# Modulation chunks in pairs, and small transfers in five parts, inside the feed-forward stage of a hybrid diffusion trunk

## What is computed

```
for l in range(2):
    mod = silu(c) @ w_ada[l] + b_ada[l]          # 6 vectors of 2048: shift, scale, gate, twice
    h = rmsnorm(x, ng[0]) * (1 + sc_a) + sh_a
    o = concat(attention, conv, rwkv of h @ w_in[l]) @ w_out[l]
    x = x + g_a * rmsnorm(o, ng[1])
    h = rmsnorm(x, ng[2]) * (1 + sc_f) + sh_f
    ff = (silu(h @ w_gate[l]) * (h @ w_up[l])) @ w_down[l]     # 2048 -> 5632 -> 2048
    x = x + g_f * rmsnorm(ff, ng[3])
```

## Time and profile before

| what | value |
|---|---|
| median of 3 runs | 3166.36 us (3164.63 to 3168.65) |
| the profiled execution, device time | 3163.59 us |
| its span, first to last instruction | 3161.8 us |
| TensorE busy | 2880.3 us, 91% |
| VectorE, ScalarE busy | 1623.6 us (51%), 1113.9 us (35%) |
| DMA, mean over the span | 190 GB/s |
| feed-forward part of layer 0 | about 822 to 1640 us of the span |
| feed-forward part of layer 1 | about 2393 to 3090 us |

### The profile page before, as it was taken

One profiled execution on the slowest core, in us unless ns is written; L12 is line 12 of the kernel. 1 busy time (PEld: TensorE's weight loads), 2 busy tenths in 40 slices (PEclk: granted clock), 3 DMA queues, 4 the chain that ended last, 5 costly groups with the idle time before them and its releaser, 6 DMA issues. The chain is left out here.

```text
span 3161.8 us, 45973 instructions
## 1 busy us (share of the span) xinstructions
PE 2880.3 (91%) x17315; PEld 2168.0 (69%) x17315; DVE 1623.6 (51%) x2108; ACT 1113.9 (35%) x1441; POOL 165.6 (5%) x209
## 2 busy tenths in 40 slices
PE   6899788889699999999996998888898999999997
PEld 1578545568577777777875885555686888888885
DVE  0465544444545445444555655455445555555555
ACT  0344322224433333333434443222244444444442
POOL 1000111110000000000001001111100000000000
PEclk9999888889899999999997999888899999999998
DMA  9765556546366667666652656666454666666662
GB/s 365 244 179 160 190 202 214 194 156 193 103 218 215 219 215 221 217 218 216 188 165 78 183 154 201 206 219 211 158 173 129 191 186 187 190 187 189 188 187 93
DMA packets 317256, 600.86 MB, mean 190 GB/s; under 512 B 23184, under 2 KB 29288, under 8 KB 316584
## 3 DMA queue, kind: packets, MB, share of 16 engines
q1 hardware_dynamic: 309488, 592.90, 59.4%
q10 hardware_dynamic: 7608, 5.60, 0.6%
HBM read 595.28 MB, written 3.15 MB: 189 GB/s over the span
## 5 line engine op out<-in xcount | busy, mean ns | idle before, releaser
L826 PE MATMUL bank<-hiW,actH 128*128 128x512 f32 (+1 forms) x2304 | 906.3, 393 | 25.4 <-DVE loW L1331 23.2
L826 PE MATMUL bank<-hiW,actL 128*128 128x512 f32 (+1 forms) x2304 | 893.5, 388 | 0.0
L826 PE MATMUL bank<-loW,actH 128*128 128x512 f32 (+1 forms) x2304 | 893.5, 388 | 0.0
L1331 DVE TENSOR_TENSOR loW<-rawW,hiW 128x1024 fp32r<-128x1024 f32 x348 | 425.6, 1225 | 448.4 <-ACT hiW L408 448.2
L408 ACT ACTIVATE hiW<-rawW 128x1024 fp32r<-128x1024 f32 x348 | 368.0, 1060 | 570.1 <-PE bank L826 558.0
L826 PEld LDWEIGHTS bank<-hiW,actH 128*128 128x128 f32 x2304 | 435.7, 189 | 154.9 <-issue 63.2
L826 PEld LDWEIGHTS bank<-hiW,actL 128*128 128x128 f32 x2304 | 435.0, 189 | 89.8
L826 PEld LDWEIGHTS bank<-loW,actH 128*128 128x128 f32 x2304 | 435.6, 189 | 85.9 <-issue 1.0
L1726 DVE TENSOR_TENSOR loW<-rawW,hiW 128x1024 fp32r<-128x1024 f32 x244 | 298.9, 1225 | 376.1 <-ACT hiW L635 376.0
L635 ACT ACTIVATE hiW<-rawW 128x1024 fp32r<-128x1024 f32 x244 | 258.4, 1059 | 486.2 <-PE bank L826 486.2
L826 PE MATMUL bank<-rawW,csR 128*32 128x512 f32 x1536 | 327.8, 676 | 82.4 <-DMA rawW<-in_w_ada 35.0
(11 more groups left out here) (255 smaller groups left out, 2272.8 us busy)
## 6 DMA issues: line engine op xcount, KB each, us to landing
rawW<-in_w_ada SPq DMA_DIRECT2D x384, 512.0 KB, 5.8
rawW<-in_w_gate SPq DMA_DIRECT2D x176, 512.0 KB, 3.7
rawW<-in_w_up SPq DMA_DIRECT2D x176, 512.0 KB, 3.7
rawW<-in_w_down SPq DMA_DIRECT2D x176, 512.0 KB, 3.7
rawW<-in_w_in SPq DMA_DIRECT2D x144, 512.0 KB, 3.6
rawW<-in_w_out SPq DMA_DIRECT2D x64, 512.0 KB, 3.6
rawW<-in_w_in SPq DMA_DIRECT2D x16, 160.0 KB, 2.3
x<-in_x_prompt SPq DMA_DIRECT2D x1, 1024.0 KB, 6.9
```

The costliest lines, as they stand in the source:

```text
L826: return pe.matmul(out, a, b, start=start, stop=stop, skip_group_check=True)
L1331: TT(loW[:, slot, :, 0:width], rawW[:, slot, :, 0:width], hiW[:, c % LEAD, :, 0:width].bitcast(F32), ALU.subtract).then_inc(lo_ready, 1)
```

## The change

The modulation chunks of a block come in twos: a pair behind every sixth chunk, in place of one behind every third. A block has four pairs in place of eight single chunks; the products, their banks and their strips stay. `place`, the order of SyncE's loads, the order of TensorE's work and the count that VectorE waits for at the block's end follow. TensorE's wait for the row copied last (`rows_out`) moves from chunk 2 to chunk 5. Apart from that, `parameters` is cut into five parts, issued in blocks 2 to 6 between the conversions of chunks 15 and 16; at the start of layer 0 all five are issued one behind the other. The rule in `high` for the chunk four conversions back names the place in the block before, where j is over 1.

```
-            return ffn_base(l, j) * 4 + i + (i // 3 if ada_in(l, j) else 0)
+            return ffn_base(l, j) * 4 + i + (2 * (i // 6) if ada_in(l, j) else 0)
...
-                            if ada_in(l, j) and i % 3 == 2:
-                                a = i // 3
-                                load(0, place(l, j, i) + 1, wnext[:, 2 * a:2 * a + 2, (j - 1) * NW:j * NW])
+                            if ada_in(l, j) and i % 6 == 5:
+                                for a in range(2 * (i // 6), 2 * (i // 6) + 2):
+                                    load(0, place(l, j, i) + 1 + a % 2, wnext[:, 2 * a:2 * a + 2, (j - 1) * NW:j * NW])
...
-            def parameters(l):
-                act.wait_ge(prm_zero, l + 1)
+            def parameters(l, part):
...
+                if part == 0:
+                    act.wait_ge(prm_zero, l + 1)
...
-                        before = place(l, j, i - LEAD) if i >= LEAD else at - LEAD
+                        before = place(l, j, i - LEAD) if i >= LEAD else place(l, j - 1, i + FFN_CHUNKS - LEAD) if j > 1 else at - LEAD
...
-                        high(j, 12, 28)
+                        high(j, 12, 16)
+                        if 2 <= j < 7:
+                            parameters(l + 1, j - 2)
+                        high(j, 16, 28)
...
-                    parameters(l)
+                    for part in range(5):
+                        parameters(l, part)
...
-                if l + 1 < LAYERS:
-                    parameters(l + 1)
                 ffn(l)
...
-                    k = (2 * c if k0 is None else k0) + n
+                    k = 2 * c + n if k0 is None else k0 + 2 * (c - c0) + n
...
-                        if i % 3 == 2 and ada_in(l, j):
-                            if i == 2:
+                        if i % 6 == 5 and ada_in(l, j):
+                            if i == 5:
                                 pe.wait_ge(rows_out, 2 + 8 + (j - 1))
-                            ada_chunks(0, at + 1, at + 2, 6, 2 * (i // 3))
+                            ada_chunks(0, at + 1, at + 3, 6, 4 * (i // 6))
...
-                        dve.wait_ge(chunk_used, place(l, j, FFN_CHUNKS - 1) + 2 + SLOTS)
+                        dve.wait_ge(chunk_used, place(l, j, FFN_CHUNKS - 1) + 3 + SLOTS)
```

More of the change, by code:

```diff
@@ L441, in norm @@
                                    tf[:, b % 2].rearrange("p (k t) -> p k t", k=4), ACT.Copy).then_inc(nt_hi, 1)
-            def parameters(l):
-                act.wait_ge(prm_zero, l + 1)
+            def parameters(l, part):
+                row = lambda ap: ap.rearrange("(r c) -> r c", c=P)
                 put = lambda dst, src: act.dma_start(dst, src).then_inc(par_rows, 16)
-                row = lambda ap: ap.rearrange("(r c) -> r c", c=P)
+                tab = lambda dst, src: act.dma_start(dst, src).then_inc(par_tabs, 16)
@@ L447, in parameters @@
                 mu = A["rwkv_mu"][l]
[L448 to L468, removed]
+                if part == 0:
+                    act.wait_ge(prm_zero, l + 1)
+                    put(prm[0:12, 0, :], row(mu[0:12 * P]))
+                    put(prm[12:13, 0, 0:64], mu[12 * P:12 * P + 64].unsqueeze(0))
+                    put(prm[13:14, 0, 0:GATE_RANK], mu[12 * P + 64:D_RWIN].unsqueeze(0))
+                    for c, name in ((COL_W0, "rwkv_w0"), (COL_A0, "rwkv_a0")):
+                        put(prm[c:c + 8, 0, :], A[name][l].rearrange("d (r c) -> (d r) c", c=P))
@@ new lines, in parameters @@
+                if part == 1:
+                    for c, name in ((COL_KK, "rwkv_k_k"), (COL_KA, "rwkv_k_a"), (COL_LG, "rwkv_ln_g"), (COL_LB, "rwkv_ln_b")):
+                        put(prm[c:c + 4, 0, :], row(A[name][l]))
+                if part == 2:
+                    put(prm[COL_RK:COL_RK + 4, 0, :], A["rwkv_r_k"][l].rearrange("(r a) b -> r (a b)", a=2))
+                    put(prm[COL_CV:COL_CV + 12, 0, :], A["conv_w"][l].rearrange("w (r c) -> (w r) c", c=P))
+                    put(prm[0:64, 1, :], A["norm_g"][l].rearrange("n (r c) -> (n r) c", c=P))
+                    put(prm[0:96, 2, :], row(A["b_ada"][l]))
@@ new lines, in parameters @@
+                if part == 3:
+                    tab(wla[0:32], A["rwkv_w_up"][l].rearrange("d r n -> r d n"))
+                    tab(wla[32:64], A["rwkv_a_up"][l].rearrange("d r n -> r d n"))
+                    tab(wg[:], A["rwkv_g_up"][l])
+                    tab(ctxk[:], A["cache_k"][0][l])
+                    tab(ctxv[:], A["cache_v"][0][l])
+                if part == 4:
+                    tab(qkw[:, 0], A["q_norm"][l].partition_broadcast(P))
+                    tab(qkw[:, 1], A["k_norm"][l].partition_broadcast(P))
+                    for d in range(2):
+                        tab(s0all[:, d], A["state_rwkv"][0][l][d].rearrange("(f h) i j -> (h i) f j", h=2))
```

## The result

The changed kernel takes 3119.3 us (median of 4 runs, 3113.4 to 3121.7), the kernel before 3165.5 beside it; the ratio is 0.9851, with a 95% interval of 0.9834 to 0.9868, so 42 to 53 us less. The prediction was 3119.5 us in a range of 3112 to 3130.

The account below looks back on a forecast made before the run. The prediction took TensorE's own stream and its interruptions to bound layer 0's feed-forward part. Savings of 37.7 us (detours) and 9.2 us (transfers), 46.9 us, took 3166.4 us to 3119.5 us, range 3112 to 3130 us.

Parts of the forecast that it names:

- The bound: Layer 0's feed-forward part: TensorE's own stream and its interruptions, one 7.4 us wait and 64 detours, set the end.
- The detours: Layer 0's feed-forward blocks: 64 single-chunk detours of 1.197 us become 32 pairs of 1.217 us, saving 37.7 us.
- case of no overlap: Rival: a pair's second chunk runs wholly behind the first, 1.05 us more; 13.9 us saved, 3152.5 us; 3 in 100.
- rows of eight: Layer 0's earlier parts: two chunks together, eight records, span 1.06 and 1.07 us; the second costs 0.01 to 0.02 us.
- The partial overlap: Rival: in each pair the second chunk is held up 0.26 us; 8.4 us lost, 3127.9 us; 5 in 100.
- The transfers: Ahead of layer 0's feed-forward part: moving 22 small DMAs into blocks 2 to 6 removes a stall, 9.2 us saved.
- What else moves: Feed-forward part's load order, row copy, residues and earlier conversions: nothing gained or lost, 0 us.
- The slower rival: A pair's own weights land late and TensorE waits; at 20 us landing 96 us lost, 3215.5 us; 2 in 100.
- The sum: Whole kernel: 37.7 + 9.2 = 46.9 us saved from the median of 3166.4 us, giving 3119.5 us.

Follow-up runs that it names:

- e3_same_strips: Changed kernel, but pairs are chunks (0,2), (1,3), (4,6), (5,7), both writing the same two strips: 3146.2 us, ratio 0.9934 to the kernel before.
- the parts alone: Changed kernel with single modulation chunks again, transfers still in five parts: 3155.6 us, ratio 0.9965 to the kernel before.
- the pairs alone: Changed kernel with the 22 transfers again in one piece ahead of the feed-forward part: 3130.3 us, ratio 0.9885 to the kernel before.
- e6_narrow: Changed kernel with modulation products of 64 columns in place of 512 inside the feed-forward part: 3095.2 us, ratio 0.9766 to the kernel before.
- e5_one_place: Changed kernel with all 22 transfers issued in block 2, between conversions of chunks 15 and 16: 3118.4 us, ratio 0.9840 to the kernel before.
- e7_octets: Changed kernel with all eight modulation chunks of a block in one detour at its end: 3191.2 us, ratio 1.0075 to the kernel before.
- e4_quads: Changed kernel with four modulation chunks behind every twelve: 3113.4 us, ratio 0.9834 to the kernel before; run again, 3111.3 us.

## Why the prediction was right

**The bound.** TensorE's stream was taken as the only limit of the stage, and it is: in the changed kernel it is busy through every block at full granted clock, and it has no wait from 845 to 1560 us.

**The detours.** 1.197 us for a single chunk stood for 64 of them; a pair was put at 1.217 and takes 1.205. The gain, 32 x (2 x 1.197 - 1.205) = 38.0 us, was put at 37.7. What made it safe was that eight such records stood in the trace of before, in another stage. That the strips are the reason, and not only that detours are half as many, was an argument there; `e3_same_strips` shows it for 27.4 of the 38.0 us. The other 10.7 us, what half as many detours save as such, the prediction did not tell apart: its case of no overlap put a second chunk at a further 1.05 us (3152.5 us in all), where 0.86 and 3146.2 were measured. Its rows of eight held both gains, so the sum was right without it. The partial overlap, some 3127 us in the estimate from the Trainium skill's 2.38 for three column tiles, does not show: the four strips take 1.07 us together where two take 1.05. The span model of the same section (TensorE: Matmul & The Clock Gate, "Measured speedup vs the span model"), some 4 ns for a further tile, is close to these rows.

**The transfers.** 9.2 us were taken from the difference between the layers; the changed kernel's own is 34.38 - 25.04 = 9.3, and the parts alone gave 0.35% (0.23 to 0.47), 11 us with 7 to 15 in the interval. With the pairs alone the stall came out at 10.7 us, more than any estimate here, since the clock stayed low for longer behind it. That the issues cost nothing in their new place was argued from 2.88 us of idle time; it is shown, and with more room than was claimed: even 9.4 us of issues are hidden there.

**What else moves** was put at 0. That holds for the time. But one sentence of that step was incomplete: that a load starts as many chunks ahead as before. It does, and yet with pairs 14 conversions wait for their load, and modulation loads land after 5.8 us instead of 4.6. A likely reason is that two modulation loads start one right behind the other, and the weights behind them share the DMA engines with both; it is not shown apart, and the pace counts too: with pairs in the same order `e3_same_strips`, whose blocks are slower, has 3 such waits, `e6_narrow`, whose blocks are faster, 17. The slower rival was on the right track, weights that come late, with the wrong weights: it was priced by a pair's own, needed 17 us later, while what comes late first are feed-forward weights. With eight chunks in a detour late weights make the kernel slower than before.

**The sum** of 46.9 us stands against 46.2 in the stage and 46.2 between the medians (3165.5 - 3119.3). So close a match is partly luck. The two terms came out at 38.0 + 9.3 = 47.4 us, and the stage's moving end took 1.2 us back in the execution profiled, where the granted clock was low for longer behind a wait that both kernels have. Between the medians the interval is 42 to 53 us.

## What to carry to other kernels

Narrow products that leave strips of the array empty are cheapest where enough of them stand together to fill all strips: here a second chunk cost 0.01 us in the other strips and 0.86 us in the same ones. When small work is bundled into a prefetched stream, look at what it does to the lead of the loads behind it: the conversions' waits for DMA (0 to 2, 11 to 14, 91 to 93 with one, two, four in a bundle) showed the limit coming before the time did. A string of DMA issues belongs into a steady stretch, where the issuing engine runs ahead of its users, and not at a stage's start; here cutting it up was then secondary.

## What the runs showed of the hardware

- ScalarE issues DMAs while it is still converting: the conversion that starts at 968.24 runs 1.06 us, and the first issue behind it starts at 968.26. The same in `e5_one_place` (972.22 and 972.24). So the first microsecond of that string of issues ran beside the conversion.
- Going from 128-column products to 32-column ones and back costs some 0.35 us at full granted clock, an estimate from two widths: with eight records of 64 columns a detour costs 0.46 us, with 512 columns 1.205. The detours saved give 0.33.
- After waits of 7 us TensorE's products ran at half rate at first: in `e7_octets` behind a wait of 7.2 us 0.43 us from one to the next at a granted clock of 0.50 (946 to 950 us), and 0.23 at 1.00 from 952 us on. Behind the wait of 1.25 us in `e4_quads` the granted clock stayed at 1.00.
